# Expert weights loaded in runs of 8 KB instead of 2 KB, and three more weight slots filled once a layer

## The reference, cut to what matters

```python
def expert_block(args):
    xb, e = args
    hdn = jax.nn.silu(xb @ w_gate[e]) * (xb @ w_up[e])     # (64, 1024) @ (1024, 512), twice
    return hdn @ w_down[e]                                 # (64, 512) @ (512, 1024)
...
y = hier_moe(xn2, ...)
h = h + gt2 * y.reshape(b, n_lat, D_MODEL)
```

## Time and profile before

| | |
|---|---|
| median of 3 runs | 3467.81 us (3464.67 to 3468.54) |
| the profiled execution | 3464.86 us, its span 3463.3 us |
| PE busy | 2808.0 us, 81% of the span |
| DVE, ACT, POOL busy | 1249.0, 848.2, 1032.6 us |
| moved by DMA | 780.63 MB, mean 225 GB/s |
| first to last store of an expert, layer 1 | 1867.50 to 2399.16 us |
| the same, layer 2 | 2901.95 to 3436.27 us |

### The profile page before, as it was taken

The page is one execution under the profiler, slowest core; times in us unless marked ns, Lnnn a source line. Parts: engine busy times, 40 slices in busy tenths (PEclk is TensorE's granted clock), DMA queues, the critical chain, the costliest instruction groups (busy, mean ns, idle before and its releaser), DMA issues.

```text
span 3463.3 us, 35386 instructions
## 1 busy us (share of the span) xinstructions
PE 2808.0 (81%) x12993; PEld 1760.4 (51%) x12993; DVE 1249.0 (36%) x2350; ACT 848.2 (24%) x1186; POOL 1032.6 (30%) x495
## 2 busy tenths in 40 slices
PE   4889879998998986899966777875797976787775
PEld 2668757677776765566652222221675652222221
DVE  2732233344215224742352222223437252232223
ACT  0243312234334112521121111112224221111111
POOL 0067656642874342222111000001372420000000
PEclk8999999999999998999988999998899988889998
DMA  7545478862454442032239999999251559999997
GB/s 298 180 130 186 152 260 290 289 233 77 155 167 151 145 160 82 14 111 86 97 110 329 374 371 373 376 376 335 74 158 32 199 183 333 372 375 368 377 374 265
DMA packets 366108, 780.63 MB, mean 225 GB/s; under 512 B 15076, under 2 KB 16274, under 8 KB 365216
## 3 DMA queue, kind: packets, MB, share of 16 engines
q1 hardware_dynamic: 337312, 669.61, 55.6%
q0 software_dynamic: 28672, 109.36, 9.3%
HBM read 733.58 MB, written 62.62 MB: 230 GB/s over the span
## 4 chain that ended last, share of the span: by engine, by line
PE 55%; DMA 17%; DVE 12%; issue 5%; SPq 4%; POOL 4%; ACT 3%; POOLq 0%; DVEq 0%; ACTq 0%
PE banks L720 9%; PE banks L725 9%; PE banks L721 9%; PE banks L1136 6%; PE banks L803 5%; PE banks L1114 5%; DMA arena<-moe_x 3%; DMA tokens_out<-in_moe_w_up 3%; SPq L592 3%; POOL weight_ring_r L1699 3%; DMA weight_ring<-in_moe_w_up 2%; DMA arena<-in_moe_w_down 2%; DMA weight_ring<-in_dil_w_qkv 1%; DMA rel_rows<-arena 1%; PE banks L853 1%
## 5 line engine op out<-in xcount | busy, mean ns | idle before, releaser
L1699 POOL TENSOR_TENSOR weight_ring_r<-weight_ring,weights_high_r 128x2048 fp32r<-128x2048 f32 x124 | 565.0, 4564 | 572.6 <-ACT weights_high_r L1358 443.3
L720 PE MATMUL banks<-weights_high_r,x_transposed_r 128*128 128x512 f32 x1008 | 407.1, 404 | 36.0 <-ACT weights_high_r L1358 11.5
L1358 ACT ACTIVATE weights_high_r<-weight_ring 128x2048 fp32r<-128x2048 f32 x124 | 234.4, 1898 | 768.5 <-PE banks L725 331.1
L1833 POOL DMA_DIRECT2D moe_y<-arena x64 | 33.8, 529 | 1035.2 <-DVE arena L2511 1019.0
L725 PE MATMUL banks<-weight_ring_r,x_transposed_r 128*128 128x512 f32 x1328 | 324.5, 391 | 3.0 <-POOL weight_ring_r L1699 3.0
L1699 POOL TENSOR_TENSOR weight_ring_r<-weight_ring,gates_r 128x2048 fp32r<-128x2048 f32 (+1 forms) x60 | 270.6, 4521 | 140.8 <-ACT gates_r L1358 79.7
L725 PEld LDWEIGHTS banks<-weight_ring_r,x_transposed_r 128*128 128x128 f32 x1328 | 248.7, 188 | 58.0 <-POOL weight_ring_r L1699 6.6
L1114 PE MATMUL banks<-weight_ring,arena 128*64 128x512 f32 x1024 | 240.9, 604 | 41.9 <-DMA weight_ring<-in_moe_w_up 25.5
L720 PEld LDWEIGHTS banks<-weights_high_r,x_transposed_r 128*128 128x128 f32 x1008 | 193.7, 192 | 93.8 <-issue 29.6
L1564 ACT ACTIVATE arena<-banks 64x1024 f32<-64x1024 f32 x64 | 65.3, 1020 | 595.6 <-PE banks L1114 595.6
L2493 DVE TENSOR_TENSOR arena<-banks,arena 64x1024 f32<-64x1024 f32 x64 | 77.8, 1216 | 352.1 <-ACT arena L1564 352.1
(11 more groups left out here) (368 smaller groups left out, 4673.9 us busy)
## 6 DMA issues: line engine op xcount, KB each, us to landing
weight_ring<-in_moe_w_gate SPq DMA_DIRECT2D x64, 1024.0 KB, 15.7
weight_ring<-in_moe_w_up SPq DMA_DIRECT2D x64, 1024.0 KB, 15.1
weights_high<-in_moe_w_down SPq DMA_DIRECT2D x64, 1024.0 KB, 16.1
x_transposed<-in_moe_w_gate SPq DMA_DIRECT2D x60, 1024.0 KB, 16.2
tokens_out<-in_moe_w_up SPq DMA_DIRECT2D x60, 1024.0 KB, 15.6
arena<-in_moe_w_down SPq DMA_DIRECT2D x60, 1024.0 KB, 16.2
weight_ring<-in_w_in SPq DMA_DIRECT2D x56, 1024.0 KB, 5.2
weight_ring<-in_w_ada SPq DMA_DIRECT2D x48, 1024.0 KB, 7.2
```

What stands on the lines that cost most here:

```text
L720: nc.tensor.matmul(banks[t][:, 0:width], xh, wh[:, k, :], start=k0 + k == 0, stop=False)
L1358: nc.scalar.activation(high(s, kn, width), slot(c, kn, width), ACT.Copy).then_inc(high_ready, 1)
L1699: nc.gpsimd.tensor_tensor(slot(c, kn, width, ring_r), slot(c, kn, width), high(s, kn, width), ALU.subtract).then_inc(low_ready, 1)
```

## The change

1. **8 KB runs.** A chunk of gate or up now takes rows 8p+4g to 8p+4g+3 for partition p (g is the half): one run of 8 KB. A chunk of down takes two whole rows, 4p+2g and 4p+2g+1: one run of 8 KB as well. So that products stay right, the turns of tokens and of hidden rows take every eighth (every fourth) column instead of 128 neighbouring ones, and down's first chunk now holds half of the rows for all columns: each half of down has four matmuls on each of the two banks.
2. **Three more slots.** `scaled_rows` (hs), the front of `gates` (GT) and a piece of the arena take one chunk each, once a layer. Two of them are filled after `route_x`, before routing is done, the third after `route_ready`. From the 16th chunk on there are 12 slots again, in another order.
3. **SP's loop** begins at expert 5 instead of 3, and the two stages before it are written out.
4. In one computation of the lambda of attention DVE uses `vector_rows` for its 64 columns instead of `scaled_rows`.

```diff
+            if n >= E_RING:
+                place, a = ((hs, 0), (GT, 0), (A, RT + 2 * P))[n - E_RING]
+                return place[:, a:a + kn * width].rearrange("p (k n) -> p k n", k=kn)
...
+                once = order[:10] + [12, 13, 10, 11, 14]
                 for n in range(6 * NE):
-                    fill(order[n % E_RING])
+                    fill(once[n] if n < len(once) else order[(n - len(once)) % E_RING])
...
-                if prev[c] is not None and (slots[c] < RING or c - prev[c] == E_RING):
+                if prev[c] is not None and (slots[c] < RING or prev[c] >= expert_chunk[0]):
...
+                elif slots[c] in (12, 13):
+                    sp.wait_ge(route_x, 2 * sum(all_tiles[:layer_now[0] + 1]))
                 elif slots[c] >= 10:
                     sp.wait_ge(route_ready, layer_now[0] + 1)
...
-                        src = I[name][layer].rearrange("e (g k p) n -> e g p k n", p=P, k=KG)
+                        src = I[name][layer].rearrange("e (p g k) n -> e g p k n", p=P, k=KG)
...
-                    src = I["moe_w_down_2"][layer].rearrange("e (k p) (g n) -> e g p k n", p=P, g=2)
-                    sp.dma_start(slot(c, KG, BANK), src[e, half]).then_inc(w_in[slots[c]], 16)
+                    src = I["moe_w_down_2"][layer].rearrange("e (p g k) n -> e g p k n", p=P, k=2)
+                    sp.dma_start(slot(c, 2, D), src[e, half]).then_inc(w_in[slots[c]], 16)
...
-                                                   A[0:CAP, E_X + par * D + k * P:E_X + par * D + (k + 1) * P],
+                                                   A[0:CAP, E_X + par * D + k:E_X + (par + 1) * D:KD],
...
-                                                   A[0:CAP, E_HD + par * 512 + k * P:E_HD + par * 512 + (k + 1) * P],
+                                                   A[0:CAP, E_HD + par * 512 + k:E_HD + (par + 1) * 512:4],
...
-                        w = slot(next_chunk(i, per_turn), KG, BANK)
-                        for k in range(4):
-                            h = A[:, E_HT + par * 256 + k * CAP:E_HT + par * 256 + (k + 1) * CAP]
-                            last = nc.tensor.matmul(halves(ps[2 + half], k), h, w[:, k, :], start=k < 2, stop=k >= 2)
+                        w = slot(next_chunk(i, per_turn), 2, D)
+                        for n in range(2):
+                            for k in range(2 * half, 2 * half + 2):
+                                h = A[:, E_HT + par * 256 + k * CAP:E_HT + par * 256 + (k + 1) * CAP]
+                                last = nc.tensor.matmul(halves(ps[2 + n], k), h, w[:, k % 2, n * BANK:(n + 1) * BANK],
+                                                        start=half == 0, stop=half == 1)
...
-                    v(tt(rows(0)[:, 0:64], brow[:, n * 128:n * 128 + 64], brow[:, n * 128 + 64:n * 128 + 128], ALU.mult))
-                    v(red(small[:, 98 + n:99 + n], rows(0)[:, 0:64], X, ALU.add), act_req if n else dve_step)
+                    v(tt(vrow[:, 0:64], brow[:, n * 128:n * 128 + 64], brow[:, n * 128 + 64:n * 128 + 128], ALU.mult))
+                    v(red(small[:, 98 + n:99 + n], vrow[:, 0:64], X, ALU.add), act_req if n else dve_step)
```

More of the change, by code:

```diff
@@ L47 @@
 E_RING = 12
+E_EXTRA = 3
 KG = 4
@@ L238, in over_down @@
         def over_down(half):
-            return spare[:, half * KG * BANK:(half + 1) * KG * BANK].rearrange("p (k n) -> p k n", k=KG)
-        w_in = [sem(f"weights_arrived_{i}") for i in range(E_RING)]
+            return spare[:, half * KG * BANK:(half + 1) * KG * BANK].rearrange("p (k n) -> p k n", k=2)
+        w_in = [sem(f"weights_arrived_{i}") for i in range(E_RING + E_EXTRA)]
         arena_free = sem("rows_and_arena_free")
@@ L605, in experts @@
                 layer_now[0] = layer
-                c0 = len(freed)
+                c0 = expert_chunk[0] = len(freed)
                 used0 = seen.now(w_used)
@@ L630, in experts @@
                 c = load_down(layer, 1, c, lambda c: take_slot(c))
[L631 to L636, removed]
+                for e in (3, 4):
+                    c = load_gate_up(layer, e, c, lambda c: take_slot(c))
+                    c = load_down(layer, e - 1, c, lambda c: take_slot(c))
+                with sp.Fori(0, 13) as i:
+                    k = load_gate_up(layer, 2 * i + 5, c, lambda c: take_slot(c, i, True))
+                    k = load_down(layer, 2 * i + 4, k, lambda c: take_slot(c, i, True))
+                    k = load_gate_up(layer, 2 * i + 6, k, lambda c: take_slot(c, i, True))
+                    load_down(layer, 2 * i + 5, k, lambda c: take_slot(c, i, True))
+                c += 13 * 12
                 c = load_gate_up(layer, NE - 1, c, lambda c: take_slot(c))
@@ L1091, in turn_x @@
                         pe.wait_ge(xg_ready, b + e + 2 * i)
-                    last = waiting_turn(ps[4][:, 0:CAP], A[0:CAP, E_X + par * D:E_X + par * D + P])
+                    last = waiting_turn(ps[4][:, 0:CAP], A[0:CAP, E_X + par * D:E_X + (par + 1) * D:KD])
                     for k in range(1, KD):
                         last = nc.tensor.transpose(ps[4][:, k * CAP:(k + 1) * CAP],
-                                                   A[0:CAP, E_X + par * D + k * P:E_X + par * D + (k + 1) * P],
+                                                   A[0:CAP, E_X + par * D + k:E_X + (par + 1) * D:KD],
                                                    ident[0:CAP, 0:CAP])
@@ L1119, in turn_hidden @@
                     pe.wait_ge(hd_ready, counted(pe, b + e + 1 + 2 * i))
-                    last = waiting_turn(ps[5][:, 0:CAP], A[0:CAP, E_HD + par * 512:E_HD + par * 512 + P])
+                    last = waiting_turn(ps[5][:, 0:CAP], A[0:CAP, E_HD + par * 512:E_HD + (par + 1) * 512:4])
                     for k in range(1, 4):
                         last = nc.tensor.transpose(ps[5][:, k * CAP:(k + 1) * CAP],
-                                                   A[0:CAP, E_HD + par * 512 + k * P:E_HD + par * 512 + (k + 1) * P],
+                                                   A[0:CAP, E_HD + par * 512 + k:E_HD + (par + 1) * 512:4],
                                                    ident[0:CAP, 0:CAP])
@@ L1169, in experts @@
                         pe.wait_ge(over["x_in"], counted(pe, 16 * j + 16))
-                        last = waiting_turn(ps[4][:, 0:CAP], A[0:CAP, E_X:E_X + P])
+                        last = waiting_turn(ps[4][:, 0:CAP], A[0:CAP, E_X:E_X + D:KD])
                         for k in range(1, KD):
                             last = nc.tensor.transpose(ps[4][:, k * CAP:(k + 1) * CAP],
-                                                       A[0:CAP, E_X + k * P:E_X + (k + 1) * P], ident[0:CAP, 0:CAP])
+                                                       A[0:CAP, E_X + k:E_X + D:KD], ident[0:CAP, 0:CAP])
                         last.then_inc(over["xT"], 1)
@@ L1183, in experts @@
                         pe.wait_ge(over["hidden"], counted(pe, j + 1))
-                        last = waiting_turn(ps[5][:, 0:CAP], A[0:CAP, E_HD:E_HD + P])
+                        last = waiting_turn(ps[5][:, 0:CAP], A[0:CAP, E_HD:E_HD + 512:4])
                         for k in range(1, 4):
                             last = nc.tensor.transpose(ps[5][:, k * CAP:(k + 1) * CAP],
-                                                       A[0:CAP, E_HD + k * P:E_HD + (k + 1) * P], ident[0:CAP, 0:CAP])
+                                                       A[0:CAP, E_HD + k:E_HD + 512:4], ident[0:CAP, 0:CAP])
                         last.then_inc(over["hiddenT"], 1)
@@ L1191, in experts @@
                             w = over_down(half)
-                            for k in range(4):
-                                last = nc.tensor.matmul(halves(ps[2 + half], k),
-                                                        A[:, E_HT + k * CAP:E_HT + (k + 1) * CAP],
-                                                        w[:, k, :], start=k < 2, stop=k >= 2)
+                            for k in range(2 * half, 2 * half + 2):
+                                for n in range(2):
+                                    last = nc.tensor.matmul(halves(ps[2 + n], k),
+                                                            A[:, E_HT + k * CAP:E_HT + (k + 1) * CAP],
+                                                            w[:, k % 2, n * BANK:(n + 1) * BANK],
+                                                            start=half == 0, stop=half == 1)
                         last.then_inc(over["down"], 1)
```

2 lines of the change are left out of this document (1 added, 1 removed).

## The result

The changed kernel takes 3625.76 us, the median of 4 runs (3623.58 to 3628.73), against 3468.18 us for the kernel before in the same rounds; the ratio is 1.0467, 95% interval 1.0452 to 1.0483. That is 157.6 us more. The forecast was 3490 us, 22 us more, with 3555 as the upper end. That the kernel would be slower was right (chance 0.53), the size was far off.

A forecast was written before the change was run, and what follows sets the result against it. A ring through POOL's store and fetch was taken to bound the kernel: 17.04 + 0.65 + 0.2 = 17.9 us a round. Layers +9.6 and +7.0, starts +5.5, together +22 us, gave 3490 us; eight in ten from 3425 to 3555.

The forecast's parts named there:

- What bounds the kernel: Among the experts: a ring of waits at 17.04 us a round first, then the weight stream at 17.83 us.
- a ring with a DMA in it: Down, copy, POOL's store and next token fetch, PE's turn, down again: 17.04 us now, 17.9 us after the change.
- The rate of the stream: SP's weight loads: 8 KB packets at 420 GB/s; with tokens and results 16.8 us an expert instead of 18.1.
- The fetch's delay: Wait before POOL's first packet: about 60 KB per engine already taken on, 2.3 to 2.7 us, unchanged by 8 KB.
- I take five packets in between instead of ten: SP's packets among those of POOL's store and fetch, fewer through stream slack: +0.65 us a round, bounds +0 and +2.2.
- No relief: Rival: the backlog before the fetch stays as deep, 19.4 us a round throughout, 3565 us; chance 0.08.
- The turn: PE's turn of tokens, loaded with 32 bytes between elements: +0.2 us in the ring, between nothing and 1.27 us.
- The ends of a layer: First three experts at 19.4 us (full backlog), last two at 13.9 us (weights landed, shorter fetch).
- The starts: Three chunks instead of two after `route_ready` delay each layer's first fetch: 2.5 and 3 us, together +5.5 us.
- the step is dear: Rival: PE's loads in the turn take twice as long, +60 us on the likeliest, 3550 us; chance 0.07.

The follow-up runs named there:

- the 4 KB loads: Kernel before with weights loaded in runs of 4 KB and nothing else: 3490.87 us, ratio 1.0082.
- The loads alone: Kernel before with weights loaded in runs of 8 KB, plain turns, 12 slots and nothing else changed: 3618.75 us, ratio 1.0461.
- the extra DMA: Kernel before with one more POOL DMA (64 rows of 4 KB into an idle buffer) ahead of each fetch from expert 2 on: 3606.0 us, ratio 1.0401.
- the kernel with the turn alone: Kernel before with turns of tokens and hidden rows taken with a step, weights loaded as before: 3463.51 us, ratio 1.0002.
- the slots alone: Kernel before with the three more weight slots and SP's written-out stages, weights in 2 KB runs: 3458.42 us, ratio 0.9983.
- the runs alone: Kernel before with 8 KB runs, turns with a step and down's new order, but 12 slots: 3618.17 us, ratio 1.0455.
- POOL's new order: POOL fetches e+2's tokens ahead of e-1's store: kernel before 3460.75 us; with 8 KB runs, 12 slots 3399.60 us; changed kernel 3386.56 us.

## Why the prediction was wrong

**What bounds the kernel** was right: a ring with a DMA in it, close behind the stream, and the chain of the changed kernel is that ring throughout.

**The rate of the stream** was right. At rest from POOL's packets the changed kernel moves 0.42 MB a us with 8 KB packets (predicted 420 GB/s); an expert's share with tokens and results was put at 16.8 us, and where the stream sets the pace again it is 17.04.

**The fetch's delay** was right: from the store's issue to the first packet it is 4 us with 2 KB and with 8 KB packets.

**The step that failed** is "I take five packets in between instead of ten". It was 12.6, ends included, and the same count in the kernel before is 12.8: there was no relief at all, and the fetch grew by 2.9 us instead of 0.65. The working before it says that PE frees down's two chunks and gate's two within 9 us of down's start and that some 3.5 us of stream are left when the store's packets come. It leaves out up's two. SP's timeline in that round (a row with x2 is two DMAs):

```profile
2109.28 2.04 SPq L607 DMA_DIRECT2D weight_ring<-in_moe_w_down  x2
2112.72 0.33 SPq L599 DMA_DIRECT2D weight_ring<-in_moe_w_gate  x1
2114.42 0.33 SPq L599 DMA_DIRECT2D weights_high<-in_moe_w_gate  x1
2117.09 0.33 SPq L599 DMA_DIRECT2D weights_high<-in_moe_w_up  x1
2118.92 0.33 SPq L599 DMA_DIRECT2D x_transposed<-in_moe_w_up  x1
```

Store and fetch are issued at 2114.05 and 2114.72, their first packets come at 2118. In those 4 us up's chunks begin to be freed: PE does not stop after down, it has gate and up still to do before it waits for the tokens. From 2109.28 to 2118 us five chunks of this round are issued, 12.5 us of transfer, and the sixth follows 0.9 us later. The slack exists (the share of 0.64 in 2108 to 2111 us), but it lies while PE is at down, where nothing is issued from 2098.39 to 2109.28 us, and not where the fetch is. No run moved these loads, so this reason is read from the trace and not shown by a run; that slack gives no relief, the 4 KB loads show as well. "No relief" among the rivals was the case that came, and it too was priced too low, at 19.4 us: 17.04 + 2.8 for the 12.6 packets instead of 2.2 for ten, and 0.6 for the turn, make 20.4 us.

**The turn** was mis-sized: +0.2 us taken, +0.6 measured, and its mechanism was wrong as well. The upper bound was that of a load with a step. The loads alone have the same longer turn with a plain load, because PE has waited longer for tokens and has the lower clock when they come. The kernel before with the extra DMA has it too, with 2 KB packets and a plain turn: 6.5 us of waiting and a turn of 1.4 us. Where the profile of before has the turn, at 2027.6 us, the clock is still 1.00. The Trainium skill ("SBUF — State Buffer", Door 1: The DMA port swizzle) says that one fp32 per line of 16 bytes is read more slowly; the kernel with the turn alone shows a load of 202 ns instead of 141, so a cost of this kind exists, but it is no part of the loss.

**The ends of a layer.** Taken: three intervals of 19.4 and two of 13.9 us. Measured: one of 17.8, then 28 of 20.49, and only the last but one falls, to 10.95. Behind store 30 PE waits for no more tokens, so this interval holds no fetch at all, and the one ahead of it (20.8) still holds a full one; the prediction had a short fetch in both.

**The starts** were taken at +5.5 us and are +8.0 from last scatter to first store. In layer 1, where they are +4.8, neither the slots alone (45.17 instead of 44.58 us) nor the runs alone (44.93) account for it; what the two do together there is left open.

Layer 1 interval by interval: 28 x (20.49 - 17.55, the mean of the same intervals before) + 1.7 for the first - 5.1 for the last two = 78.9 us, which is the 610.6 - 531.7. This only says where the time lies; the prediction had 9.6 us there.

**The chances.** "No relief" had 0.08 and "the step is dear" 0.07. They had to be thought of together with a third point that no case held: a fetch that takes longer makes PE wait longer, and the wait costs clock.

## What to carry to other kernels

In these runs a small transfer that someone waits for passes the packets of a large stream about one for one, so larger packets buy the stream some per cent of rate and charge the small transfer for every one of its own packets: look first for a small DMA in the chain of waits. If there is one, take it off the chain before the stream is made faster; here that is a change of order by one expert, worth nothing by itself and 2.1% with the larger packets and slots. Do not count on slack in a stream by its mean share: look at the stream's issue times for whether it falls at the time of the small transfer (here it did not).

## What the hardware did that I had not expected

- **The wait costs clock, and the next work pays.** In the kernel with the 8 KB loads alone PE stood still from 2106.85 us on, and at 2113.1 us the granted clock was 0.50: the plain turn took 1.41 us instead of 0.87.
- **A load of PE with a step does not follow the clock as a plain one does.** Plain: 141 ns at the high clock, 221 at the low. With 32 bytes between elements: 202 and 203 ns. The step costs 0.6 us a turn at the high clock (1.42 instead of 0.87) and next to nothing at the low one (1.47 and 1.41).
- **The stream slows the fetch more once it is no longer behind.** With 4 KB packets the fetch took 7.2 us while the stream was catching up and 8.3 us once it had. With 8 KB packets it took 8.3 us with POOL's new order, where the stream is behind, and 9.6 us in the changed kernel, where it is not.
- **The delay of the first packet** stayed at 4 us with 2 KB and with 8 KB packets (medians 3.9 and 4.2): what is ahead of it is a volume (or a time), not a number of packets.
- **Packets of both queues take longer in the second half of their time together.** In the changed kernel a packet of SP's takes 0.29 us of an engine in 2118 to 2120 us and 0.46 us in 2121 to 2123 us, in the kernel before 0.085 us in 2110 to 2111 us and 0.15 us in 2111.5 to 2113 us. No run tells why.
